# Attention in a two-block network: one scaling of the product with the values per group of query blocks, instead of one of the probabilities per block

## The reference

```python
def attend(q, k, v):
    b, nq = q.shape[:2]
    qg = q.reshape(b, nq, N_KV_HEADS, Q_PER_KV, HEAD_DIM)
    s = jnp.einsum('bqhgd,bkhd->bhgqk', qg, k).astype(jnp.float32) * ATTN_SCALE
    p = jax.nn.softmax(s, axis=-1).astype(v.dtype)
    o = jnp.einsum('bhgqk,bkhd->bqhgd', p, v)
    return o.reshape(b, nq, N_Q_HEADS * HEAD_DIM)
```

## Time and profile before

| | us |
|---|---|
| median of the runs | 2199.31 |
| the profiled execution | 2195.83 |
| its span | 2193.9 |
| mixers of layer 0, from first scores on | 145 to 271 |
| mixers of layer 1 | 962 to 1060 |

### The profile page before, as it was taken

The page is one execution under the profiler, slowest core; times in us unless marked ns, Lnnn a source line. Parts: engine busy times, 40 slices in busy tenths (PEclk is TensorE's granted clock), DMA queues, the critical chain, the costliest instruction groups (busy, mean ns, idle before and its releaser), DMA issues.

```text
span 2193.9 us, 27688 instructions
## 1 busy us (share of the span) xinstructions
PE 2116.8 (96%) x10852; PEld 1748.0 (80%) x10852; DVE 1310.5 (60%) x1897; ACT 841.4 (38%) x1362; POOL 639.7 (29%) x330
## 2 busy tenths in 40 slices
PE   9998899999999999989999999999999999999898
PEld 6885688989899998865778888877788888788656
DVE  5988587777787778997765522265231444532272
ACT  5334426414244244535452222242372222334552
POOL 0000003332223233200444444454234444323402
PEclk9999999999999999999999999999999999989999
DMA  8312141242423324222434232335223333311401
GB/s 329 111 56 94 68 154 39 70 142 90 132 87 102 120 82 139 87 82 91 131 94 151 79 114 86 99 94 152 69 69 95 97 98 98 92 55 57 139 1 58
DMA packets 68656, 219.56 MB, mean 100 GB/s; under 512 B 8112, under 2 KB 14000, under 8 KB 67376
## 3 DMA queue, kind: packets, MB, share of 16 engines
q1 hardware_dynamic: 66080, 212.08, 30.4%
q10 hardware_dynamic: 2448, 5.72, 0.8%
HBM read 210.17 MB, written 2.10 MB: 97 GB/s over the span
## 4 chain that ended last, share of the span: by engine, by line
PE 81%; DVE 10%; ACT 4%; issue 3%; POOL 1%; DMA 0%; POOLq 0%; DVEq 0%; ACTq 0%
PE prod L879 54%; PE prod L950 7%; PE misc L950 5%; DVE conv_acc L2677 2%; PE prod L1080 1%; PE misc L969 1%; PE prod L1161 1%; PE prod L1216 1%; PE prod L1129 1%; PE misc L1394 1%; PE misc L1067 1%; PE prod L1044 1%; POOL wlo L855 1%; PE misc L1240 1%; DVE stat L2604 1%
## 5 line engine op out<-in xcount | busy, mean ns | idle before, releaser
L855 POOL TENSOR_TENSOR wlo<-ring,whi 128x1024 fp32r<-128x1024 f32 (+4 forms) x232 | 493.7, 2128 | 1243.6 <-ACT whi L1491 1243.4
L879 PE MATMUL prod<-operand_hi,whi 128*128 128x512 f32 (+1 forms) x1416 | 507.4, 379 | 6.0 <-POOL operand_lo L824 3.4
L879 PE MATMUL prod<-operand_hi,wlo 128*128 128x512 f32 (+1 forms) x1416 | 501.1, 375 | 0.0
L879 PE MATMUL prod<-operand_lo,whi 128*128 128x512 f32 (+1 forms) x1416 | 500.4, 374 | 0.0
L1491 ACT ACTIVATE whi<-ring 128x1024 fp32r<-128x1024 f32 (+4 forms) x259 | 245.2, 947 | 498.0 <-PE prod L879 470.0
L879 PEld LDWEIGHTS prod<-operand_hi,whi 128*128 128x128 f32 x1416 | 253.7, 188 | 62.9 <-POOL operand_lo L824 5.8
L879 PEld LDWEIGHTS prod<-operand_hi,wlo 128*128 128x128 f32 x1416 | 253.3, 188 | 48.4
L879 PEld LDWEIGHTS prod<-operand_lo,whi 128*128 128x128 f32 x1416 | 253.3, 188 | 46.9
L879 PE MATMUL prod<-hidden_hi,whi 128*128 128x512 f32 (+1 forms) x528 | 188.3, 357 | 2.3 <-DVE hidden_lo L2479 0.9
L879 PE MATMUL prod<-hidden_lo,whi 128*128 128x512 f32 (+1 forms) x528 | 187.9, 356 | 0.0
L879 PE MATMUL prod<-hidden_hi,wlo 128*128 128x512 f32 (+1 forms) x528 | 186.7, 354 | 0.0
(11 more groups left out here) (443 smaller groups left out, 3660.5 us busy)
## 6 DMA issues: line engine op xcount, KB each, us to landing
ring<-in_w SPq DMA_DIRECT2D x226, 512.0 KB, 3.6
modw<-in_wmod SPq DMA_DIRECT2D x68, 512.0 KB, 3.7
ring<-in_w SPq DMA_DIRECT2D x32, 384.0 KB, 4.0
ring<-in_w SPq DMA_DIRECT2D x32, 320.0 KB, 2.9
mod_pair<-in_wpair SPq DMA_DIRECT2D x8, 1024.0 KB, 16.5
ring<-in_wmod SPq DMA_DIRECT2D x12, 512.0 KB, 4.3
dft<-in_dftx SPq DMA_DIRECT2D x8, 512.0 KB, 5.1
resid<-in_xt SPq DMA_DIRECT2D x4, 768.0 KB, 7.2
```

Of the source, the lines that this page charges most:

```text
L855: nc.gpsimd.tensor_tensor(wlo_of(j)[:, 0:w], ring[PLACE["panel", j] % RING][:, 0:w], whi_of(j)[:, 0:w].bitcast(F32), ALU.subtract).then_in ...
L879: mm = pe.matmul(G[b][:, t0:t0 + tn], w[:, k * P:(k + 1) * P], a[:, t0:t0 + tn], start=(i == 0 and q == 0), stop=(i == g.kc - 1 and q == 2))
```

## The change

- The exponentials' sums go into a tile `sums` of their own, a column per pair, block and head. The probabilities are no longer scaled.
- At an end VectorE inverts the sums of the whole group in one instruction (`invert_sums`). ScalarE spreads the inverses over 64 columns each (`spread_inverse`, before the copy of the last chunk), TensorE transposes the result block by block into `M1` (`turn_inverse`, before the last product with the values), and ScalarE copies it to a tile `shares` (`copy_share`, behind the next exponentials). VectorE multiplies the bank `MM` by it (`scale_weighed`, behind the next maxima and the opening steps). The upper and the lower half are then made from `shares`.
- TensorE's first transposition of a pair waits for the exponentials instead of the scaled probabilities, and after an end also for the copy of the share; its first product with the values waits for the scaling and no longer for the lower half. ScalarE's `end` waits for the scaling instead of the last product.
- The maxima come out negated, so the small negation is gone; the factor 0.125 is put into the gain of q's norm once at the start.

```diff
                     if c == 0:
-                        pe.wait_ge(pair_probs, before + i + 1)
+                        pe.wait_ge(pair_exp, 2 * (before + i) + 2)
+                    if c == 0 and i - 1 in ends:
+                        pe.wait_ge(share_copied, ended(i - 1))
                     wait(pe, pair_copied, at)
...
                         t = qb * pairs[i][4] + (first + q // 2) * P
...
                     if c == 0 and i - 1 in ends:
-                        pe.wait_ge(operand_lo, ops + order["end", i - 1] + 1)
+                        pe.wait_ge(weighed_scaled, ended(i - 1))
...
@@ -1242,6 +1258,14 @@
                                        probs_t[at % 3][:, q * P:(q + 1) * P], start=(first == 0 and q < 2),
                                        stop=(first == nk // P - 2 and q > 1))
                     mm.then_inc(pair_weighed, 1)
+
+                def turn_inverse(i):
+
+                    pe.wait_ge(inverse_spread, ended(i))
+                    pe.wait_ge(pair_copied, chunk_base(l, i + 1))
+                    for b in range(ends[i][2] // P):
+                        mm = pe.transpose(M1[:, b * P:(b + 1) * P], shares[ended(i) % 2][:, b * P:(b + 1) * P], ident)
+                    mm.then_inc(inverse_turned, 1)
...
+                    if i in ends:
+                        turn_inverse(i)
                     weigh(i, c)
...
                             ins = nc.scalar.activation(W[2 * (i % 2) + a][:, t:t + nk], S[:, 1024 * a + t:1024 * a + t + nk], ACT.Exp,
-                                                       bias=stat[:, 8 + u:9 + u], scale=0.125, accum_out=stat[:, 16 + u:17 + u])
+                                                       bias=stat[:, 8 + u:9 + u],
+                                                       accum_out=sums[:, sum_column(l, i, qb, a):sum_column(l, i, qb, a) + 1])
...
                 def end(i):
                     if i in ends:
                         h, q0, qn = ends[i]
-                        act.wait_ge(pair_weighed, chunk_base(l, i + 1))
-                        nc.scalar.activation(XH[:, h // 2, q0:q0 + qn], MM[:, 0:qn], ACT.Copy).then_inc(operand, 1)
+                        act.wait_ge(weighed_scaled, ended(i))
+                        nc.scalar.activation(XH[:, h // 2, q0:q0 + qn], shares[ended(i) % 2][:, 0:qn], ACT.Copy).then_inc(operand, 1)
+
+                def spread_inverse(i):
+                    if i in ends:
+                        k, at = ends[i][2] // 64, 8 * (ended(i) - 1 - 4 * l)
+                        act.wait_ge(inverse_ready, ended(i))
+                        nc.scalar.activation(shares[ended(i) % 2][:, 0:64 * k].rearrange("p (k f) -> p k f", k=k),
+                                             inverse[:, at:at + k].unsqueeze(2).broadcast_to([P, k, 64]), ACT.Copy).then_inc(inverse_spread, 1)
+
+                def copy_share(i):
+                    if i in ends:
+                        act.wait_ge(inverse_turned, ended(i))
+                        nc.scalar.activation(shares[ended(i) % 2][:, 0:ends[i][2]], M1[:, 0:ends[i][2]],
+                                             ACT.Copy).then_inc(share_copied, 1)
...
                     for c in range(len(pieces(pairs[i]))):
                         at = chunk_base(l, i) + c
+                        if c == len(pieces(pairs[i])) - 1:
+                            spread_inverse(i)
                         act.wait_ge(pair_turned, at + 1)
                         wait(act, pair_weighed, at - 2)
                         nc.scalar.activation(probs_t[at % 3][:, :], M1[:, :], ACT.Copy).then_inc(pair_copied, 1)
                         between(i, c)
                     if i + 1 < len(pairs):
                         exps(i + 1)
+                    copy_share(i)
...
                     dve.wait_ge(pair_scores, before + i + 1)
                     for a in range(2):
                         u = 4 * (i % 2) + nq * a
-                        link(nc.vector.tensor_reduce(stat[:, u:u + nq], S[:, 1024 * a:1024 * a + nq * nk].rearrange("p (b t) -> p b t", b=nq),
-                                                     AX.X, ALU.max))
-                        nc.vector.tensor_scalar(stat[:, 8 + u:8 + u + nq], stat[:, u:u + nq], -0.125, None, ALU.mult).then_inc(pair_negmax, 1)
-
-                def norms(i):
-                    _, _, nq, _, nk = pairs[i]
-                    for a in range(2):
-                        u = 4 * (i % 2) + nq * a
-                        dve.wait_ge(pair_exp, 2 * (before + i) + a + 1)
-                        link(nc.vector.reciprocal(stat[:, 24 + u:24 + u + nq], stat[:, 16 + u:16 + u + nq]))
-                        for qb in range(nq):
-                            t = W[2 * (i % 2) + a][:, nk * qb:nk * qb + nk]
-                            ins = nc.vector.tensor_scalar(t, t, stat[:, 24 + u + qb:25 + u + qb], None, ALU.mult)
-                    ins.then_inc(pair_probs, 1)
+                        nc.vector.tensor_reduce(stat[:, 8 + u:8 + u + nq], S[:, 1024 * a:1024 * a + nq * nk].rearrange("p (b t) -> p b t", b=nq),
+                                                AX.X, ALU.max, negate=True).then_inc(pair_negmax, 1)
...
+                def invert_sums(i):
+                    if i in ends:
+                        at = 8 * (ended(i) - 1 - 4 * l)
+                        dve.wait_ge(pair_exp, 2 * (before + i) + 2)
+                        nc.vector.reciprocal(inverse[:, at:at + ends[i][2] // 64], sums[:, at:at + ends[i][2] // 64]).then_inc(inverse_ready, 1)
+
+                def scale_weighed(i):
+                    if i in ends:
+                        share = shares[ended(i) % 2][:, 0:ends[i][2]]
+                        dve.wait_ge(share_copied, ended(i))
+                        dve.wait_ge(pair_weighed, chunk_base(l, i + 1))
+                        nc.vector.tensor_tensor(share, MM[:, 0:ends[i][2]], share, ALU.mult).then_inc(weighed_scaled, 1)
...
                 def end(i):
                     if i in ends:
                         h, q0, qn = ends[i]
-                        low_operand(XL[:, h // 2, q0:q0 + qn], MM[:, 0:qn], XH[:, h // 2, q0:q0 + qn])
+                        dve.wait_ge(weighed_scaled, ended(i))
+                        low_operand(XL[:, h // 2, q0:q0 + qn], shares[ended(i) % 2][:, 0:qn], XH[:, h // 2, q0:q0 + qn])
 
                 tops(0)
                 for i in range(len(pairs)):
-                    norms(i)
+                    invert_sums(i)
                     if i + 1 < len(pairs):
                         tops(i + 1)
                     between(i, "a")
+                    scale_weighed(i - 1)
                     end(i - 1)
                     beside(i)
                     for c in range(3):
                         between(i, c)
                     behind(i)
+                scale_weighed(len(pairs) - 1)
                 end(len(pairs) - 1)
...
+            for l in range(2):
+                nc.vector.tensor_scalar(pa(f"qg{l}"), pa(f"qg{l}"), 0.125, None, ALU.mult).then_inc(q_scaled, 1)
```

More of the change, by code:

```diff
@@ L281, in chunk_base, with sum_column @@
     return (28 if l else 0) + sum(len(pieces(pair)) for pair in pairs1(l)[:i])
+def sum_column(l, i, qb, a):
+    return 8 * sum(e < i for e in pair_ends(l)) + 2 * (pairs1(l)[i][1] % NX // P + qb) + a
 def pair_ends(l):
@@ L462, in build_program @@
         endB = top[0]
+        shares_at = region + 2 * HID * NT * 4 + 6 * 4 * HN * 4 + 4 * 4 * P * 4
+        shares = [at(f"shares{s}", NX, F32, shares_at + 4 * NX * s) for s in range(2)]
+        sums = at("sums", 32, F32, shares_at + 8 * NX)
+        inverse = at("inverse", 32, F32, shares_at + 8 * NX + 128)
         root_copy = at("root_copy", NX, F32, zone + 4 * DC * P)
@@ L584, in build_program @@
             sem("ft_ready"), sem("ft_copied"), [sem(f"dft_landed{s}") for s in range(6)], sem("dft_used"), sem("fy_copied"))
-        pair_scores, pair_negmax, pair_exp, pair_probs, pair_turned, pair_copied, pair_weighed = (
-            sem("pair_scores"), sem("pair_negmax"), sem("pair_exp"), sem("pair_probs"), sem("pair_turned"), sem("pair_copied"),
+        pair_scores, pair_negmax, pair_exp, pair_turned, pair_copied, pair_weighed = (
+            sem("pair_scores"), sem("pair_negmax"), sem("pair_exp"), sem("pair_turned"), sem("pair_copied"),
             sem("pair_weighed"))
+        q_scaled, inverse_ready, inverse_spread, inverse_turned, share_copied, weighed_scaled = (
+            sem("q_scaled"), sem("inverse_ready"), sem("inverse_spread"), sem("inverse_turned"), sem("share_copied"), sem("weighed_scaled"))
         mp_ready, rb_ready, turned, turn_copied = sem("mp_ready"), sem("rb_ready"), sem("turned"), sem("turn_copied")
@@ L1115, in mixers, with ended @@
                 ops, before, nb, fb = OPS[f"mix{l}"], 10 * l, width // P, 6 * l
+                def ended(i):
+                    return 4 * l + sorted(ends).index(i) + 1
                 reader = [(bank_free[0], RANK[g.j0 + 12])] * 2
@@ L2724, in _ @@
```

(1 more changed line is left out.)

## The result

The changed kernel takes 2206.86 us, the median of 4 runs (2206.63 to 2208.67), against 2197.97 us (2194.21 to 2199.99, 4 runs) of the kernel before on the same chip: 1.004 of it, 95% interval 1.0028 to 1.0053. It is slower by 8.9 us; 2207 was forecast. The profiled execution took 2206.74 us (span 2204.9, 11.0 more than before).

The account below looks back on a forecast made before the run. TensorE, busy 96% of the span, was taken as the bound. Gains -1.9, transposes +2.1, serial waits +5.4 and clock +2.3 made +7.9 us on the 2199.31 median: 2207, own range 2204 to 2211, overall 2198 to 2214.

Parts of the forecast that it names:

- Gains: Mixers: TensorE no longer waits for scaled probabilities in two places, and maxima come sooner in five: about -1.9 us.
- Transposes: Four added TensorE transposes of the spread inverse at each of six ends, two ends covered: +2.1 us.
- ScalarE's copies: ScalarE's 12 new copies, 6 spreads and 6 shares at the ends, fit its idle time: 0 us.
- The spread stands where it waits for a transposition: At each end, ScalarE's spread of the inverse was claimed to fall into idle time, costing 0.
- the bound of 7 us: Upper limit for ScalarE's 12 new copies if their cover failed, each costing its 0.6 us; 0 was taken.
- Serial ends: Layer 0 pairs 5 and 6, layer 1 pair 5: ScalarE's end waits for scaling queued behind maxima, delaying copies: +5.4 us.
- the 0.1 at layer 1's end: The output product's last chunk at layer 1's end needs a lower half now 0.8 us later: 0.1 us.
- The clock: Half clock behind new TensorE waits: 1.5 us at layer 0 pair 5, 0.8 at layer 1 pair 5: +2.3 us.
- Rival A: Serial ends in the mixers without more of the half clock: +3 to +6 us, 2204; chance 0.24.
- C: ScalarE becomes the bound, its 12 new copies delaying copies and exponentials: +15 us, 2214; chance 0.12.
- B: Relief of VectorE's queue wins if scaling is ready before ScalarE's first chunk copy: -5 us, 2194; chance 0.08.
- D: Everything added falls into TensorE's existing 25.5 us of idle time: within 2 us of before; chance 0.08.

Follow-up runs that it names:

- Experiment 4: Kernel before with only the maxima negated and 0.125 folded into q's gain, probabilities still scaled: 2196.64 us, ratio 0.9988.
- experiment 6: Changed kernel with VectorE's scaling ahead of the next maxima and the spread of the inverse ahead of the second chunk's copy: 2193.29 us, ratio 0.9976.
- experiment 1: Changed kernel with one line moved, VectorE's scaling of an end's product ahead of the next pair's maxima: 2197.24 us, ratio 0.9992.
- experiment 2: Changed kernel with ScalarE's upper half of an end moved behind the second chunk's copy, scaling still behind the maxima: 2198.68 us, ratio 0.9996.
- experiment 3: Changed kernel with dummy matmuls in layer 0's pair 5 wait and ahead of layer 1's sum of squares: 2206.37 us, ratio 1.0035.
- Experiment 8: Changed kernel with dummy matmuls in all three waits (layer 0 pairs 5 and 6, layer 1 pair 5): 2204.36 us, ratio 1.0026.
- experiment 9: Changed kernel with fewer dummy matmuls, only in the waits of layer 1's pair 5: 2204.77 us, ratio 1.0031.
- experiment 7: Kernel before without any scaling of the probabilities and nothing in its place, output not normalised: 2198.41 us, ratio 1.0001.

## Why the prediction was right

The sign and the mechanism were right, and the total was close; the waits were put too high, the clock and the gains too low, and the cost of the spreads was missed. Point by point:

- **Gains, forecast -1.9.** The places named show -0.5 (pair 4 of layer 0) and -0.3 to -0.4 in five segments (layer 0's pairs 7 and 8; layer 1's pairs 1, 2 and 6): about -2.3. Experiment 4 says that the part of the maxima was put too low, at 0.2 us a place and 5 places where nine stretches move.
- **Transposes, +2.1, ScalarE's copies, 0.** Pair 4 shows +0.57 = 0.63 (the transposes) - 0.5 + 0.45; pairs 9 and 10 +1.34 = 0.9 + 0.45; layer 1's last +0.66, as forecast. The 0.45 are the spreads of the first and third end. "The spread stands where it waits for a transposition" was wrong: it starts when the transposition ends, and the copy stands behind it. (At pair 4 ScalarE had just made a copy for another mixer, so there was no idle time ahead of it.) It cost 0.9 to 1.0 us, shown by experiment 6; of the bound of 7 us little came.
- **Serial ends, +5.4.** Between a pair's first scores and the product (in layer 1 the third transposition) that ends its wait, before and after: 4.56 and 6.27 us, less 0.46 for the second transposition at half clock (1.12 for 0.66), so +1.25 where 1.6 was forecast; 5.15 and 6.20, +1.05 for 1.4; and in layer 1 5.87 and 7.89, +2.0 for 2.35. With the 0.1 at layer 1's end, which no run shows by itself, 4.4 us: each hand-over was right in kind, and each wait came out 0.35 us shorter than forecast. Experiments 1 and 2 show the cause from either side: the stalls go when the scaling is early, and also when it stays late but no copy stands behind it.
- **The clock, +2.3.** This is the term that was most mis-sized. What the three segments have left beside their waits is 1.56 + 1.61 + 1.76 = 4.9 us. The first was put at 1.5 and experiment 3 measured 1.56. The second was put at nothing, "there the clock fell already": the fall there became longer, 10.2 for 6.8 us, and 24 sums of one column, now wholly inside it, took 5.28 us; before they began 1.2 us ahead of it and took 4.18. The third was given an even chance of the short stretch; the long one came. Experiment 8 bears out the first two, and the stretch behind the third transposition the third: 6.27 us at half clock, 4.48 and 4.49 at full clock in experiments 8 and 9.
- **The sum**: -2.3 + 2.1 + 0.9 + 4.4 + 4.9 = 10.0, the mixers' 10.1. Forecast were 7.9, by stretch about 5 and 3; the stretches grew by 6.7 and 3.4. That the median rose by 8.9 only, close to 7.9, owes something to luck: what lies outside the mixers takes from 1973 to 1980 us in the profiles of all these kernels, with no edit there. And that 2207 was met to 0.1 us is luck too: the forecast started from 2199.31, while the kernel before took 2197.97 beside the change, so the start was 1.3 us too high and the rise 1.0 too low.
- **The chances.** They were added up carelessly: slower is 0.40 + 0.12 = 0.52, not 0.53, and within 0.3% is 0.08 + 0.24 + 0.08 = 0.40, not 0.38. Rival A's own sum, without more of the half clock, is 5.6 us, so nearer 2205 than 2204. Neither changes the forecast.
- **The rivals.** C fell to experiment 1, B to experiment 7, D to the result; A is refuted, for layer 0 by experiments 3 and 8, for layer 1 by the time behind the third transposition. B's condition, a scaling ready before ScalarE reaches the copy, could have been arranged: experiments 1 and 6 did, and came out level with the kernel before and 0.24% faster. That is far from B's 5 us, and the negated maxima alone (experiment 4) bring 0.12%. What the scaling behind the product brings in the right order, the negated maxima apart, no run isolates.

## What to carry to other kernels

A small instruction that takes its place in a busy engine's queue passes that queue's delay to every engine whose in-order stream waits for it: before moving work from many places to one, look what stands ahead of the producer and what stands behind the consumer; here one line of order was worth 9.6 us. Removing the 24.5 us of scalings was worth nothing that could be measured, removing the 5.6 us of negations, which stood ahead of things that others waited for, about 2. A new wait of a few microseconds on TensorE cost about twice its length here (4.3 us of waits, 4.9 of clock); allow for that where the clock may fall behind it, and also where it has fallen before. When work is removed from an engine off the path, first leave it out altogether and time that: it bounds the gain as long as the order stays.

## What was not expected of the hardware

- **A fall's length changes without an edit.** Pair 6 of layer 0 is the same in the changed kernel and in experiments 3 and 9; the half clock in it lasted 10.2, 13.7 and 13.7 us and the segment took 18.67, 19.74 and 19.79. Filling the waits of both pairs left 3.4 us of it. A kernel that differs in one wait shows other falls far away (at 1988 us, or from 245 in experiment 7), each worth some 1.6 us where it could be read, which is part of what looks like noise between two kernels. The Trainium skill ("TensorE: Matmul & The Clock Gate", What's actually happening) says that the window of the activity monitor runs freely, so that one kernel starts up differently from run to run; the traces agree with that in so far as the unedited pair 6 of layer 0 took 18.67 and 19.79 us.
- **Small products lose as much as large ones in a fall.** The product of 512 columns took 3.39 us at half clock for 1.98. The 24 sums with one column each took 5.28 us, all at half clock (220 ns each); in layer 1, 16 of them at full clock took 1.84 us (115 ns each).
- **A negated maximum costs nothing more.** Two reductions over 768 columns with the sign turned take 1.82 us together, where the pair with a separate negation took 0.96 + 0.95 and 156 ns after each.
